# One norm with one root between two transformer blocks, and another order for the tail of a side thread

## The reference, cut to what matters

```python
def rms_norm(x, g):                       # end of block 1, EPS = 1e-6
    y = x * lax.rsqrt(mean(x * x) + EPS)
    return y * g
def layer_norm_2(x, g, b):                # start of block 2, NORM_EPS = 1e-5
    mu = mean(x); var = mean(square(x - mu))
    return (x - mu) * lax.rsqrt(var + NORM_EPS) * g + b
x = first_block(...)                      # ... lat + g2 * moe_ffn(h2); return rms_norm(lat, g_final)
x_lat = layer_norm_2(x, ln_in_g, ln_in_b)
x_ctx = layer_norm_2(ctx, ln_in_g, ln_in_b)
...
# layer 1 (the last), context side: nkc, nvc, ckvc, krc of split(hc @ w_in), then
mla_kc, mla_vc = mla_keys_values(ckvc, krc, g_kv, w_uk, w_uv, None)   # rms_norm_2 of ckvc, two products
```

## Time and profile before

| what | value |
|---|---|
| three runs | 2718.01, 2724.62, 2727.05 us, median 2724.62 |
| profiled execution | span 2724.3 us; no other time of this execution is given, and it lies 0.3 us below the median |
| mean granted TensorE clock | 0.974 |
| TensorE, VectorE, ScalarE, GpSimd busy | 93%, 41%, 18%, 8% of the span |
| first matmul of slot `d17` | at 1569.33 us |
| first matmul of `f0` | at 1629.80 us |

### The profile page before, as it was taken

The page is one execution under the profiler, slowest core; times in us unless marked ns, Lnnn a source line. Parts: engine busy times, 40 slices in busy tenths (PEclk is TensorE's granted clock), DMA queues, the critical chain, the costliest instruction groups (busy, mean ns, idle before and its releaser), DMA issues.

```text
span 2724.3 us, 39998 instructions
## 1 busy us (share of the span) xinstructions
PE 2547.2 (93%) x16144; PEld 1860.4 (68%) x16144; DVE 1125.1 (41%) x2652; ACT 482.0 (18%) x1042; POOL 225.3 (8%) x266
## 2 busy tenths in 40 slices
PE   6999999899999998999999779999999999999998
PEld 3565545557667765667666346669899866798998
DVE  1455114321112143110011241667687716676876
ACT  2132013221111022000000121431200114312101
POOL 0000000000000000000011000002122100020221
PEclk9989999999999999999999889999999999999999
DMA  9868999999997678999999962414544544245440
GB/s 405 341 255 360 420 410 415 418 398 412 418 418 302 278 299 347 419 419 418 418 415 417 420 244 109 143 69 180 233 170 159 212 171 143 83 166 215 157 155 17
DMA packets 121782, 779.74 MB, mean 286 GB/s; under 512 B 13248, under 2 KB 16960, under 8 KB 37888
## 3 DMA queue, kind: packets, MB, share of 16 engines
q1 hardware_dynamic: 94976, 684.76, 62.2%
q0 software_dynamic: 22560, 82.32, 7.8%
q10 hardware_dynamic: 4064, 10.09, 1.0%
HBM read 771.35 MB, written 5.77 MB: 285 GB/s over the span
## 4 chain that ended last, share of the span: by engine, by line
PE 78%; DMA 11%; DVE 8%; ACT 2%; issue 1%; SPq 0%; ACTq 0%; DVEq 0%
PE bank L726 76%; DMA ring<-in_stream 10%; PE bank L1149 1%; DMA work<-in_stream 1%; DVE MX L2387 1%; PE bank L730 1%; DVE work L2406 1%; DVE work L2289 1%; DVE bank L2389 0%; SPq L585 0%; DVE X L2328 0%; ACT work L1804 0%; DVE A L2994 0%; DVE work L2993 0%; DVE A L2995 0%
## 5 line engine op out<-in xcount | busy, mean ns | idle before, releaser
L726 PE MATMUL bank<-A,work 128*128 128x128 f32 (+1 forms) x2864 | 511.8, 329 | 12.4 <-DMA work<-in_stream 8.0
L726 PE MATMUL bank<-A,ring 128*128 128x128 f32 (+1 forms) x3088 | 508.1, 316 | 14.7 <-ACT A L1814 5.8
L726 PEld LDWEIGHTS bank<-A,work 128*128 128x128 f32 x2864 | 444.1, 193 | 72.3 <-issue 34.9
L726 PEld LDWEIGHTS bank<-A,ring 128*128 128x128 f32 x3088 | 449.6, 193 | 57.1 <-issue 12.2
L726 PE MATMUL bank<-work 128*128 128x128 f32 (+2 forms) x2704 | 402.3, 319 | 23.3 <-ACT work L1705 8.0
L726 PE MATMUL bank<-ring,A 128*32 128x512 f32 (+3 forms) x2272 | 366.2, 611 | 30.7 <-DMA ring<-in_stream 29.1
L726 PEld LDWEIGHTS bank<-work 128*128 128x128 f32 (+1 forms) x2704 | 319.6, 177 | 82.4 <-issue 38.0
L726 PE MATMUL bank<-work,ring 128*128 128x128 f32 (+1 forms) x1696 | 295.3, 323 | 1.6 <-DVE work L2410 1.6
L726 PEld LDWEIGHTS bank<-ring,A 128*32 128x32 f32 (+2 forms) x2272 | 116.6, 124 | 259.0 <-issue 203.3
L726 PEld LDWEIGHTS bank<-work,ring 128*128 128x128 f32 x1696 | 260.1, 194 | 22.0 <-DVE work L2410 2.1
L677 POOL DMA_DIRECT2D work<-in_stream x148 | 80.0, 541 | 1304.7 <-PE bank L726 1209.6
(11 more groups left out here) (334 smaller groups left out, 1918.0 us busy)
## 6 DMA issues: line engine op xcount, KB each, us to landing
ring<-in_stream SPq DMA_DIRECT2D x652, 1024.0 KB, 15.5
work<-in_stream POOLq DMA_DIRECT2D x140, 512.0 KB, 9.0
spill<-work ACTq DMA_DIRECT2D x6, 512.0 KB, 8.6
work<-in_stream POOLq DMA_DIRECT2D x8, 384.0 KB, 7.8
work<-spill POOLq DMA_DIRECT2D x6, 512.0 KB, 5.0
X<-in_xt ACTq DMA_DIRECT2D x1, 2048.0 KB, 13.3
work<-spill POOLq DMA_DIRECT2D x2, 768.0 KB, 11.8
tab_sb<-in_tab_a ACTq DMA_DIRECT2D x1, 1120.0 KB, 9.5
```

The lines of the kernel that those rows point to most:

```text
L726: return pay(pe.matmul(o, w, x, start=start, stop=stop, tile_position=place), tells)
```

## The change

It merges the two norms, reorders the tail of the side thread, and moves the steps between slots.

```diff
-    "d17": 1, "final_b": 3, "final_c": 5,
+    "d17": 5, "final_b": 1, "final_c": 9,
@@ side_order (banks)
-    ... run("nk1", "AAAA") + run("nv1", "AA") + run("low1", "DD") + [(("var", "ckv1"), "A")] + run("mk1", "AAAA") + run("mv1", "DD")
+    ... run("nk1", "AAAA") + run("low1", "DD") + [(("var", "ckv1"), "A")] + run("nv1", "AA") + run("mk1", "AAAA") + run("mv1", "DD")
-    if _key[0] == "turn":
+    if _key[0] == "turn" or _key == ("var", "ckv1"):
         _bank = 7
@@ QUARTERS
-for _stage, _tiles in (("l1_na", range(64, 128, QTILES)), ("l1_low", (16, 24)), ("l1_up", (16, 24))):
+for _stage, _tiles in (("l1_na", range(64, 96, QTILES)), ("l1_low", (16, 24)), ("l1_na", range(96, 128, QTILES)), ("l1_up", (16, 24))):
@@ TensorE, side thread (behind nk1; low1 now stands first)
-                for blk in range(TB):
-                    clinear(("nv1", blk), 512, ..., KD, after=(lambda k: free("l1_na", 96 + 4 * k + 4)) if blk else None)
-                    yield
...
+                b = [cgroup("nv1", blk) for blk in range(TB)]
+                for k in range(KD):
+                    for blk in range(TB):
+                        m = mm(b[blk][:, :], cA[:, k, blk * P:(blk + 1) * P], ctile("l1_na", 96 + 4 * k, 4), k == 0, k == KD - 1, ...)
+                    free("l1_na", 96 + 4 * k + 4)
+                    yield
+                    if k == 0:
+                        pe.wait_ge(c_sq, 6)
+                        mm(cgroup("var", "ckv1")[:, 0:T], ones, cLOW[:, 0, :], True, True, tells=True).then_inc(c_lin, 1)
+                        yield
@@ TensorE, norm between the blocks
+            def final_sums():
+                base = NBASE["final"]
+                def square(k):
+                    pe.wait_ge(sq_ready, base + k + 1)
+                    mm(bank[6][:, 0:T], ones, SQ[:, (base + k) % 2, 0:T], k == 0, False, tells=True).then_inc(sq_used, 1)
+                for k in range(KD):
+                    pe.wait_ge(res_added, 4 * (2 * UNITS - 1) + k // 2 + 1)
+                    m = mm(bank[1][:, 0:T], GAINS(k), X[:, k, 0:T], k == 0, k == KD - 1, tells=k == KD - 1)
+                    if k == KD - 1:
+                        m.then_inc(sum_ready, 1)
+                    if k:
+                        square(k - 1)
+                square(KD - 1)
@@ TensorE, last unit, before the fourth spreading pair
+                    if r == 3 and U + 1 == 2 * UNITS:
+                        wait_ctx(pe, "var", "ckv1")
@@ TensorE, main
-            norm("final", T)
+            final_sums()
             beside("final_b")
-            pe.wait_ge(mid_ready, NMID["final"] + KD)
-            norm("ln_in", T, mean=True)
+            (eight sums of squares into bank 6, added to those of final_sums)
             beside("final_c")
@@ ScalarE: low1's square and the root of var ckv1 come in slot d17, the copies of nv1 and the two
@@ sends to DRAM behind its last chunk; in the norm
-            squares("final", T, lambda k: X[:, k, 0:T], come=...)
+            for k in range(KD): (waits as before)
+                act.activation(SQ[:, (base + k) % 2, 0:T], X[:, k, 0:T], ACT.Square, scale=EPS2 ** 0.5).then_inc(sq_ready, 1)
@@ VectorE: reciprocal and scaling of cLOW come in slot d17, the copy into cA[rot] behind nv1; in the norm
-                link(dve.tensor_scalar(MEAN[:, 0:w], bank[6][:, 0:w], 1.0 / D, None, ALU.mult))
                 for k in range(KD):
-                    dve.tensor_tensor(X[:, k, 0:w], X[:, k, 0:w], MEAN[:, 0:w], ALU.subtract).then_inc(xc_ready, 1)
+                    dve.wait_ge(sq_ready, NBASE["final"] + k + 1)
+                    dve.scalar_tensor_tensor(X[:, k, 0:T], X[:, k, 0:T], par_("gf", k, 1), bank[1][:, 0:T], ALU.mult, ALU.subtract)
+                       .then_inc(xc_ready, 1)
+                beside("final_b")
-            norm("final", ...)                       # reciprocal and 8 scalings
-            for k in range(KD): ... sum_up(k, T)     # 7 additions
@@ VectorE, second mixture, ahead of its units
+                    for k in range(KD):
+                        dve.tensor_scalar(GAINS(k), ones, par_("gf", k, 1), 1.0 / D, ALU.mult, ALU.mult)
```

More of the change, by code:

```diff
@@ L219, in side_order @@
         out += [(("ffg", j), "A"), (("ffu", j), "D")]
-    return out + run("down", "D" * KD) + [(("mean", "ln2"), "D"), (("var", "ln2"), "A")] + run("nk1", "AAAA") + run("nv1", "AA") \
-        + run("low1", "DD") + [(("var", "ckv1"), "A")] + run("mk1", "AAAA") + run("mv1", "DD")
+    return out + run("down", "D" * KD) + [(("mean", "ln2"), "D"), (("var", "ln2"), "A")] + run("nk1", "AAAA") + run("low1", "DD") \
+        + [(("var", "ckv1"), "A")] + run("nv1", "AA") \
+        + run("mk1", "AAAA") + run("mv1", "DD")
 SGROUP, STAKER, STAKEN, SBANK, SBEFORE = {}, [], [], [], []
@@ L1059, in seven, with norm @@
                     used()
-            def norm(name, w, mean=False):
+            def norm(name, w):
                 K, base = NCHUNK[name], NBASE[name]
-                if mean:
-                    pe.wait_ge(xsum_ready, NMEAN[name] + 1)
-                    mm(bank[6][:, 0:w], ones, XSUM[:, 0:w], True, True, tells=True).then_inc(sum_ready, 1)
                 for k in range(K):
@@ L1758, in context @@
                     yield
[L1759 to L1765, removed]
                 yield from steps(2)
@@ L1768, in context @@
                 act.activation(cLOW[:, 0, :], cLOW[:, 2, :], ACT.Square).then_inc(c_sq, 1)
+                yield
                 act.activation(cMEAN, ctake("var", "ckv1")[:, 0:T], ACT.Sqrt, bias=EPS[:, 1:2], scale=1.0 / P)\
                    .then_inc(c_taken["A"], 1)
+                yield
+                yield from steps(KD - 2)
+                for blk in range(TB):
+                    act.activation(cV[:, blk, :], ctake("nv1", blk), ACT.Copy).then_inc(c_taken["A"], 1)
+                wait_ctx(act, "nv1", 1)
+                act.dma_start(saved[:, 0:1024].rearrange("p (a b) -> p a b", b=T), cNK).then_inc(c_spilled, 16)
+                act.dma_start(saved[:, 1024:2048].rearrange("p (a b) -> p a b", b=512), cV).then_inc(c_spilled, 16)
                 yield
@@ L2025, in _ @@
             moe(1)
-            squares("final", T, lambda k: X[:, k, 0:T],
-                    come=lambda k: act.wait_ge(res_added, 4 * (2 * UNITS - 1) + k // 2 + 1))
+            base = NBASE["final"]
+            act.activation(OPEN[:, :], EPS[:, 0:1], ACT.Sqrt)
+            for k in range(KD):
+                act.wait_ge(res_added, 4 * (2 * UNITS - 1) + k // 2 + 1)
+                if base + k >= 2:
+                    act.wait_ge(sq_used, base + k - 1)
+                act.activation(SQ[:, (base + k) % 2, 0:T], X[:, k, 0:T], ACT.Square, scale=EPS2 ** 0.5).then_inc(sq_ready, 1)
             beside("final_b")
@@ L2263, in context @@
                 yield from norm("ln2", ("ln2_g", 0, KD), ("ln2_b", 0, KD), 0, 8, 1)
-                yield from steps(4 + TB)
+                yield from steps(4)
                 for j in range(2):
@@ L2274, in context @@
                 yield
+                yield from steps(KD - 1)
+                ctake("nv1", 1)
+                wait_ctx(dve, "low1", 1)
+                dve.tensor_copy(cA[rot, :, :], cLOW[rot, 3:4, :].broadcast_to([32, KD, T])).then_inc(c_kr, 1)
                 yield from steps(2)
@@ L2826, in _ @@
             moe(1)
-            norm("final", T, lambda k: X[:, k, 0:T], lambda k: X[:, k, 0:T], [(0, T, lambda k: par_("gf", k, 1))])
-            for k in range(KD):
-                dve.wait_ge(mid_ready, NMID["final"] + k + 1)
-                sum_up(k, T)
-            beside("final_b")
             layer_norm("ln_in", ("lni_g", 0, KD), ("lni_b", 0, KD), 0, 0, 8)
```

59 lines of the change are left out of this document (27 added, 32 removed).

## The result

| | before | after |
|---|---|---|
| median | 2723.46 us (4 runs, 2718.01 to 2727.05) | 2706.11 us (4 runs, 2700.97 to 2707.49) |
| ratio | | 0.9939, 95% interval 0.9923 to 0.9954 |
| profiled execution | span 2724.3, clock 0.974 | 2706.95 us, span 2705.2, clock 0.978 |
| first matmul of `d17` to first of `f0` | 1569.33 to 1629.80 = 60.47 us | 1571.22 to 1614.19 = 42.97 us |

The change is faster by 0.6%: 17 us, forecast 17.0.

A forecast was written before the change was run, and what follows sets the result against it. TensorE's in-order list with its waits, not the norm, was taken to bound the passage from d17 to f0. Terms summed to 43.5 against 60.47 us, a gain of 17.0, giving 2707.3 us; range 2700 to 2716.

The forecast's parts named there:

- low1 and the new wait in d17: Start of d17: low1's 16 products, 7.07 us, then 0.6 us until VectorE empties the bank nv1 needs.
- two chunks, var, spreading products: Rest of d17 on TensorE: two nv1 chunks 3.52 us, var 0.44, last spreading products 3.56.
- final_sums: Merged norm's 16 products, GAINS and ones in turn: streamed price 7.04 us, bounds 8.45 as a chain and 9.9.
- mk1 and mv1: Last products before f0: 5.28 us if nothing waits, 7.21 before the change, taken as 5.8.
- and not the norm: Ahead of f0: TensorE's list ends last; f0 began 11.7 us after ScalarE had written all of A.
- What is removed: First root, reciprocal, scalings, additions, one matmul, the mean: costed at nothing under cover, some 9 us without it.
- the spare is 7.6 us: In final_c: A is whole about 7 us in, so f0 does not wait for it, with 7.6 us to spare.
- Rival 4: Longer d17 delays the norm, which ends last if it takes 7.6 us more; 2713 at upper bounds; chance 0.05.
- The table load: In d17: var's root needs a 1.28 us load; nothing added by the rows, about 1 us by the page.
- Rival 1: Last quarter comes late or d17 waits for one: up to 1.5 us, 2709 to 2711 with GAINS; chance 0.08.
- Rival 2: Gain given back behind f0, where something does not move with TensorE: 2716 if half, 2724 if all; chance 0.08.
- Rival 3: Clock falls to 0.50 in the layer norm's sparse sums, final_c can double: 2722, up to 2736; chance 0.06.

The follow-up runs named there:

- norm only: The changed kernel with the merged norm kept but the side thread's tail back in its old order and slots; ratio to before 0.9999, passage 60.31 us.
- Mean by vector: The changed kernel with VectorE adding the chunks times gain and one TensorE product for the mean in place of eight; passage 41.63 us, ratio to before 0.9942.
- tail only: The changed kernel with its new tail and slots kept but the two separate norms put back; ratio to before 0.9976, passage 52.66 us.
- norm longer: The changed kernel with two more reciprocals of 1.75 us each in VectorE's part of the norm, written to an unread tile; passage 46.76 us.
- Tail late: New tail with the old two norms, but five chunks of nv1 in `final_b` (slots 5, 5, 5); ratio to before 0.9959, passage 50.52 us.
- slack five: The changed kernel with four more chunks of values ahead of the sums of the layer norm (slots 5, 5, 5); passage 50.55 us.
- the two split kernels: Tail late and slack five with only ScalarE's list reordered, nv1's copies and sends ahead of A's first write; passages 47.58 and 46.48 us.
- values by block: The changed kernel with nv1 in two groups of eight products, one per 128 tokens, not quarter by quarter (slots 3, 1, 5); passage 43.99 us.
- slack all: The changed kernel with the whole rest of the side thread ahead of the sums of the layer norm (slots 5, 10, 0); passage 48.70 us.

## Why the prediction was right, point by point

| step of the sum | predicted | measured |
|---|---|---|
| low1 and the new wait in d17 | 7.07 + 0.6 | 7.73 |
| two chunks, var, spreading products | 3.52 + 0.44 + 3.56 | 7.40 |
| final_sums | 7.04 (bounds to 9.9) | 6.91 |
| chunk in `final_b` | 1.76 | 1.71 |
| sums of the layer norm | 4.93 | 4.66 |
| five chunks | 8.79 | 8.62 |
| mk1 and mv1 | 5.8 | 5.94 |
| d17 to f0 | 43.5 | 42.97 |

**What bounded it.** TensorE's in-order list, with waits that other work could fill. Right in the main: norm only, with three of the four waits in place, gains 0.2 us; the changed kernel, with none, gains 17.5. But the prediction added "and not the norm", and gave as the reason of the 7.29 us that nothing was left to do. The row names another, `<-ACT work L1768`: var waited for low1's square, and ScalarE made that square as the eighth write of A ended (1614.07 + 4.04 = 1618.11; the two records overlap by 0.1):

```profile
1618.02 0.40 ACT L1768 ACTIVATE work<-work 128x256 f32<-128x256 f32 x1
```

VectorE had copied out the group of low1 that it squares by 1601.41 (not shown). So in the kernel before, too, the norm held TensorE through ScalarE's list, and by var's root and reciprocal it held mk1 for the 2.89 us as well. The change was right in that it takes this square, the root and the reciprocal out from behind the norm into d17.

**final_sums.** The streamed price was the open choice (7.04 against 8.45 or 9.9). Between GAINS products TensorE never waited: final_sums is one run of products, and it was ScalarE that waited for TensorE, 0.45 us ahead of a square (the row at 1588.77). Mean by vector shows the other price, 0.58 us a sum, where no such product stands between.

**What is removed was costed at nothing, about 9 us without its cover.** Both shown: norm only 0.2 us, and tail only, where one chunk of 1.71 us is left as cover, stands 7.53 us.

**The step that failed: "the spare is 7.6 us".** It was read off f0, the only product that needs A. But A holds more than f0: ScalarE copies nv1 behind A, and mk1 waits for that copy. The spare is 1.04 us (norm longer). Tail late and slack five, argued from the 7.6, missed by 4.5 us and more, and the two split kernels show that the list on ScalarE makes the wait. The rows of the kernel before had shown such a step behind A, the square above. The forecast did not suffer because the norm's length was right: A was whole 7.1 us into `final_c`, as predicted. With 1.04 us to spare in place of 7.6 that is in part luck: a norm 3.54 us longer than it was already cost 3.79 us (norm longer), where the prediction counted on nothing. Rival 4, a norm that ends last, would have begun 1 us above the count, and its condition was stated wrongly.

**The table load.** The prediction had var's root need a load of 1.28 us. It needed none: the root ran at 1581.38 and the load followed at 1581.87. A load for an earlier root of the side thread stands at 1527.94 in the changed kernel, and between the two ScalarE ran only copies, the writes of that norm and low1's square. The later load belongs to the code behind the branch that ends the second mixture, and is made again there although a root had just run without one. This is in line with the Trainium skill (ScalarE activation tables: per-element evaluation and per-set limits, section Table sets in the compiler and the runtime), where loads are placed block by block; that a branch is what parted the blocks here is only argued. The drain of 1.38 us beside a load at a change of table set (the Trainium skill, ScalarE: Activation LUTs, section What ACT_TABLE_LOAD costs), by which the prediction would have been about 1 us longer, does not show. Behind the load at 1581.87 the next activation starts at 1583.17, 0.02 us after its end at 1583.15; that load follows a root, so it need not be a change of set. The load at 1527.94 stands between a Silu and a root: the Silu ends at 1527.92, the load at 1529.22, and the root starts at 1529.23.

**Rival 1, late quarters.** No pause behind a transfer is left in the passage. The last quarter, issued at 1602.67, landed after 4.7 us, sooner than the 7.2 to 12.1 of the sum; even values by block, with its last two quarters issued later than here, lost only 0.37 us to them.

**Rival 2, given back behind f0.** Not so: f0 to the end is 3.5 us shorter, by the clock of single executions. Over all kernels run it lay between 1090.6 (norm only) and 1095.4 us (tail only).

**Rival 3, the clock.** It stayed at 1.00 in the sparse sums (windows above), as the prediction argued from the earlier trace rows. In the passages of the experiments it fell behind TensorE's pauses of 2.31, 2.50, 3.59, 5.79 and 7.53 us (0.50 to 0.78 in a stretch of 4 us behind them); the rows behind pauses of 0.65, 1.32 and, in slack all, 1.71 us show 1.00. The length of one pause does not settle it: 0.64 and 0.50 stood behind the pause of 1.59 us at 523 in the changed kernel, 1.00 behind the same pause in the kernel before, and the 0.66 at 1806.40 in the kernel before came behind pauses of 0.93 and 0.79 us, where the changed kernel kept 1.00 behind 0.69 and 0.79.

**The median.** 2706.11 against 2707.3: the terms were 0.5 us too long together, and the rest is within the spread of the runs. The four runs span 6.5 us, so that the two agree to 1.2 is chance; the passage, 42.97 against 43.5, is the better test.

## What to carry to other kernels

Where an engine works an in-order list through waits, gain comes from putting ready work into each wait, and two edits can be worth little apart and much together, because the one takes away the cover that the other makes needless: price each step with and without its cover. The spare of a chain is not read at its last consumer alone; look through the list of every engine on it for work that stands behind it (here copies that free a bank), and for who waits for that. Where single spans scatter, time the passage between two landmarks on either side of the edit.

## What the runs showed of the hardware

- The same code got different granted clocks in different executions, 0.88 to 0.98 between 100 and 200 us, and d17 began anywhere from 1561.5 to 1573.8: a spread of 12 us ahead of the passage.
- A pause of TensorE can be paid twice: behind one of 2.50 us the next 20 records took 7.10 us instead of 5.94, with the clock at 0.67 in the 4 us around their start; behind one of 1.32 us it stayed at 1.00.
- "Issue" as the end of a pause need not mean that nothing was waited for: at 1612.36 in tail late it was the bank that ScalarE had just read, and with those copies moved up the pause was gone.
